# Operands of the experts' second product exchanged: activations stationary, 512 columns of the expert matrix moving, results added straight into the residual

## The reference

```python
def peer_ffn(x, wq, subkeys, u, v):
    ...
    def expert_block(args):
        xs, es, gs = args
        h = jax.nn.gelu(jnp.einsum('td,thkd->thk', xs, u[es], preferred_element_type=jnp.float32), approximate=False)
        return jnp.einsum('thk,thkd->td', gs * h, v[es].astype(jnp.float32)).astype(x.dtype)
    ...

def trunk_layer(...):
    ...
    h = h + mixed @ lp['w_out']
    h = h + peer_ffn(rms_norm(h, lp['norm2_g']), lp['peer_wq'], lp['peer_subkeys'], lp['peer_u'], lp['peer_v'])
```

## Time and profile before

| | |
|---|---|
| median of 3 runs | 5353.5 us (5353.49 to 5354.45) |
| the profiled execution: its own time, and its span | 5357.1 us, 5355.3 us |
| TensorE matmul (PE), weight loads (PEld) | 89%, 86% of the span |
| VectorE (DVE), ScalarE (ACT), GpSimd (POOL) | 59%, 31%, 7% |
| mean granted clock of TensorE, share of full speed | 0.942 |
| second product's matmuls: each of the three passes | 3584 into `ex_op` and 512 into `ex_hp` |
| adds of its outputs on VectorE (L2301) | 896 and 128, 754 ns each |

### The profile page before, as it was taken

One profiled execution on the slowest core, in us unless ns is written; L12 is line 12 of the kernel. 1 busy time (PEld: TensorE's weight loads), 2 busy tenths in 40 slices (PEclk: granted clock), 3 DMA queues, 4 the chain that ended last, 5 costly groups with the idle time before them and its releaser, 6 DMA issues. The chain is left out here.

```text
span 5355.3 us, 99808 instructions
## 1 busy us (share of the span) xinstructions
PE 4784.8 (89%) x39364; PEld 4585.4 (86%) x39364; DVE 3141.2 (59%) x6341; ACT 1671.9 (31%) x2570; POOL 363.5 (7%) x194
## 2 busy tenths in 40 slices
PE   7767697899999999999887676969999999999998
PEld 7647496899999999999885464969899999999998
DVE  3554578884555555557735644788755555555576
ACT  2322232882222222222222222228722222222222
POOL 0200054000000000000002000540000000000000
PEclk9878798999999999999988787989999999999999
DMA  3330121565333333335323301216743322333253
GB/s 96 111 140 1 54 90 53 174 198 191 115 115 127 126 115 115 129 113 177 125 78 126 117 0 71 90 44 179 214 162 125 128 115 115 128 125 115 104 196 120
DMA packets 390832, 631.24 MB, mean 118 GB/s; under 512 B 29184, under 2 KB 327680, under 8 KB 348800
## 3 DMA queue, kind: packets, MB, share of 16 engines
q1 hardware_dynamic: 388640, 620.74, 33.0%
q10 hardware_dynamic: 2016, 8.26, 0.4%
HBM read 526.52 MB, written 152.36 MB: 127 GB/s over the span
## 5 line engine op out<-in xcount | busy, mean ns | idle before, releaser
L228 PE MATMUL ex_op<-ex_ah,ex_vl 128*128 128x288 f32 x3584 | 1062.9, 297 | 7.4 <-DVE ex_acc L2301 6.4
L230 PE MATMUL ex_op<-ex_ah,ex_vh 128*128 128x288 f32 x3584 | 1058.7, 295 | 0.0
L229 PE MATMUL ex_op<-ex_al,ex_vh 128*128 128x288 f32 x3584 | 1057.8, 295 | 0.0
L2301 DVE TENSOR_TENSOR ex_acc<-ex_acc,ex_op 128x576 f32<-128x576 f32 x896 | 672.7, 754 | 549.2 <-PE ex_op L230 549.2
L228 PE MATMUL ex_hp<-x_hi,ex_ul 128*128 128x288 f32 x3072 | 906.9, 295 | 19.1 <-PEq L122 15.8
L230 PE MATMUL ex_hp<-x_hi,ex_uh 128*128 128x288 f32 x3072 | 907.3, 295 | 0.0
L229 PE MATMUL ex_hp<-x_lo,ex_uh 128*128 128x288 f32 x3072 | 906.6, 295 | 0.0
L228 PEld LDWEIGHTS ex_op<-ex_ah,ex_vl 128*128 128x128 f32 x3584 | 673.9, 188 | 14.9 <-DVE ex_acc L2301 14.9
L230 PEld LDWEIGHTS ex_op<-ex_ah,ex_vh 128*128 128x128 f32 x3584 | 674.1, 188 | 0.0
L229 PEld LDWEIGHTS ex_op<-ex_al,ex_vh 128*128 128x128 f32 x3584 | 673.9, 188 | 0.0
L2250 ACT ACTIVATE ex_vh<-ex_v 128x2048 fp32r<-128x2048 f32 x128 | 245.5, 1918 | 1139.6 <-PE ex_op L230 860.1
(11 more groups left out here) (414 smaller groups left out, 8842.7 us busy)
## 6 DMA issues: line engine op xcount, KB each, us to landing
ex_u<-in_peer_uT SPq DMA_DIRECT2D x128, 1024.0 KB, 7.7
ex_v<-in_peer_v SPq DMA_DIRECT2D x128, 1024.0 KB, 6.8
gate_matrix<-g_stage SPq DMA_DIRECT2D x18, 4096.0 KB, 15.9
ex_g<-gate_matrix SPq DMA_DIRECT2D x128, 576.0 KB, 5.0
dec_k<-in_cache_kT SPq DMA_DIRECT2D x16, 1536.0 KB, 9.7
dec_v<-in_cache_v SPq DMA_DIRECT2D x16, 1536.0 KB, 6.8
out_s_k<-in_cache_k_kept SPq DMA_DIRECT2D x128, 190.5 KB, 6.2
out_s_v<-in_cache_v_kept SPq DMA_DIRECT2D x128, 190.5 KB, 6.2
```

The source lines that it names most:

```text
L228: nc.tensor.matmul(out, w_lo, x_hi, start=first, stop=False)
L229: nc.tensor.matmul(out, w_hi, x_lo, start=False, stop=False)
L230: return nc.tensor.matmul(out, w_hi, x_hi, start=False, stop=last)
L2301: nc.vector.tensor_tensor(a, a, o[:, :, 0:HALF], ALU.add).then_inc(s.added, 1)
```

## The change

The activations become the stationary operand and V moves, 512 columns at a time. An output is now one tile of 128 tokens by 512 features: 2 expert blocks x 3 passes, 6 matmuls into one bank. There are 10 outputs per group (`OUTS`): 5 token tiles x 2 halves of the features. The last tile has 64 tokens only. For it, the low and the high part stand side by side as 128 stationary columns (`a_lo_hi`), so one matmul forms low x high in rows 0 to 63 and high x high in rows 64 to 127 of the bank, and a second, with 64 stationary columns, adds high x low to rows 0 to 63: 4 matmuls per output instead of 6. ScalarE copies the 64 columns of the high part once more for this (one more instruction per block).

VectorE adds each output, 128 x 512, directly into `h`; rows 64 to 127 of the last tile of `h` serve as the second accumulator and are set to zero at the start, in place of `acc`. At the end SyncE moves those rows to a scratch tile `lower`, and VectorE adds it to rows 0 to 63. The closing stage with its transposes is gone. The outputs go round through the four banks of `op` in both halves; `late_product` is gone, and `hp` is no longer used for outputs.

```diff
--- before.py
+++ after.py
@@ -2110,23 +2110,30 @@
 
 
     NR = NG - EARLY
+    BANKS = 4
+    OUTS = 2 * NT
     with ExitStack() as ctx:
         def sb(name, shape, dt=F32):
             return ctx.enter_context(sbuf(nc, name, shape, dt))
 
-        acc = sb("ex_acc", [P, KD, T])
+        lower = sb("ex_lower", [TS_, D])
         u_raw = [m.u_raw0, sb("ex_u", [P, KD, EG * P])]
         u_hi, u_lo = m.u_hi, m.u_lo
         early = [u[:].rearrange("p k c -> p (k c)")[:, 0:EG * T].rearrange("p (e t) -> p e t", e=EG) for u in u_raw]
         v_raw, v_hi, v_lo = (sb("ex_v" + n, [P, 2, EG, D], dt) for n, dt in (("", F32), ("h", F32R), ("l", F32R)))
         gb = sb("ex_g", [P, 2, NU, EG, UNIT])
         a_raw = sb("ex_a", [P, EG, T])
-        a_hi, a_lo = (sb("ex_a" + n, [P, 2, EG, T], F32R) for n in "hl")
+        a_hi, a_lo_hi = sb("ex_ah", [P, 2, EG, T], F32R), sb("ex_al", [P, 2, EG, T + TS_], F32R)
+        a_lo = a_lo_hi[:, :, :, 0:T]
         hp = ctx.enter_context(psum(nc, "ex_hp", [P, EG, 2, 512], F32))
-        op = ctx.enter_context(psum(nc, "ex_op", [P, 2, 2, 512], F32))
-        banks = (op[:, 0], op[:, 1], hp[:, 0], hp[:, 1])
+        op = ctx.enter_context(psum(nc, "ex_op", [P, BANKS, 512], F32))
+
+        def bank(j, n):
+
+            return (j * OUTS + n) % BANKS
+
         names = ["u_in0", "u_in1", "v_in0", "v_in1", "g_in0", "g_in1", "kept", "uh", "ul", "vh", "vl", "h_made",
-                 "gelud", "gated", "ah", "al", "out_made", "added", "zeroed", "early_in0", "early_in1"]
+                 "gelud", "gated", "ah", "al", "out_made", "added", "early_in0", "early_in1", "folded"]
         with stage(nc, *names) as (block, s):
             u_in, v_in, g_in = (s.u_in0, s.u_in1), (s.v_in0, s.v_in1), (s.g_in0, s.g_in1)
             early_in = (s.early_in0, s.early_in1)
@@ -2172,6 +2179,8 @@
                         load(i * 2 + j, j)
                 for f in range(EARLY):
                     load_early(f, f % 2)
+                sp.wait_ge(s.added, NG * OUTS)
+                sp.dma_start(lower[:], m.h[TS_:P, NT - 1, :]).then_inc(s.folded, 16)
                 sp.wait_ge(s.kept, 32 * NG)
 
             @block.tensor
@@ -2193,15 +2202,22 @@
                 def second_product(g, j, first=False):
                     pe.wait_ge(s.al, g * EG + EG)
                     pe.wait_ge(s.vl, g + 1)
-                    for n in range(KD):
-                        if not (first and n < 2):
-                            pe.wait_ge(s.added, g * KD + (n - 1))
-                        for half in range(2):
-                            t = slice(half * HALF, (half + 1) * HALF)
-                            c = slice(n * P, (n + 1) * P)
+                    for n in range(OUTS):
+                        i, c, q = n // 2, slice(n % 2 * 512, (n % 2 + 1) * 512), bank(j, n)
+                        t = slice(i * P, i * P + ROWS[i])
+                        if not (first and n < BANKS):
+                            pe.wait_ge(s.added, g * OUTS + (n - BANKS + 1))
+                        if i < NT - 1:
                             for e in range(EG):
-                                ins = three_passes(nc, op[:, n % 2, half, 0:HALF], v_hi[:, j, e, c], v_lo[:, j, e, c],
-                                                   a_hi[:, j, e, t], a_lo[:, j, e, t], e == 0, e == EG - 1)
+                                ins = three_passes(nc, op[:, q, :], a_hi[:, j, e, t], a_lo[:, j, e, t],
+                                                   v_hi[:, j, e, c], v_lo[:, j, e, c], e == 0, e == EG - 1)
+                        else:
+                            for e in range(EG):
+                                both = (op[:, q, :], a_lo_hi[:, j, e, TP_:T + TS_], v_hi[:, j, e, c])
+                                low = (op[0:TS_, q, :], a_hi[:, j, e, t], v_lo[:, j, e, c])
+                                first_e, last_e = (both, low) if e == 0 else (low, both)
+                                nc.tensor.matmul(*first_e, start=e == 0, stop=False)
+                                ins = nc.tensor.matmul(*last_e, start=False, stop=e == EG - 1)
                         ins.then_inc(s.out_made, 1)
 
                 first_product(0, 0, True)
@@ -2214,26 +2230,9 @@
                     second_product(i * 2, 0)
                 second_product(NR - 1, 1)
 
-                def late_product(g, j, first=False):
-
-                    pe.wait_ge(s.al, g * EG + EG)
-                    pe.wait_ge(s.vl, g + 1)
-                    for n in range(KD):
-                        if not (first and n in (2, 3)):
-                            pe.wait_ge(s.added, g * KD + (n - (1 if first and n < 2 else 3)))
-                        for half in range(2):
-                            t = slice(half * HALF, (half + 1) * HALF)
-                            c = slice(n * P, (n + 1) * P)
-                            for e in range(EG):
-                                ins = three_passes(nc, banks[n % 4][:, half, 0:HALF], v_hi[:, j, e, c], v_lo[:, j, e, c],
-                                                   a_hi[:, j, e, t], a_lo[:, j, e, t], e == 0, e == EG - 1)
-                        ins.then_inc(s.out_made, 1)
-
-                late_product(NR, 0, True)
-                late_product(NR + 1, 1)
-                with pe.Fori(NR // 2 + 1, NG // 2) as i:
+                with pe.Fori(NR // 2, NG // 2) as i:
                     for j in range(2):
-                        late_product(i * 2 + j, j)
+                        second_product(i * 2 + j, j)
 
             @block.scalar
             def _(act):
@@ -2246,11 +2245,12 @@
                 def split_v(g, j, turn, first=False):
                     act.wait_ge(v_in[j], turn * 16 + 16)
                     if not first:
-                        act.wait_ge(s.out_made, g * KD - KD)
+                        act.wait_ge(s.out_made, g * OUTS - OUTS)
                     nc.scalar.activation(v_hi[:, j], v_raw[:, j], ACT.Copy).then_inc(s.vh, 1)
 
                 def high(g, j, e):
                     act.wait_ge(s.gated, g * EG + (e + 1))
+                    nc.scalar.activation(a_lo_hi[:, j, e, T:T + TS_], a_raw[:, e, TP_:T], ACT.Copy)
                     nc.scalar.activation(a_hi[:, j, e, :], a_raw[:, e, :], ACT.Copy).then_inc(s.ah, 1)
 
                 def step(g, j, turn, first=False, last=False):
@@ -2293,12 +2293,11 @@
                     nc.vector.tensor_tensor(v_lo[:, j], v_raw[:, j], v_hi[:, j].bitcast(F32),
                                             ALU.subtract).then_inc(s.vl, 1)
 
-                def add(g, ns, late=False):
+                def add(g, j, ns):
                     for n in ns:
-                        dve.wait_ge(s.out_made, g * KD + (n + 1))
-                        a = acc[:, n, :].rearrange("p (a t) -> p a t", a=2)
-                        o = banks[n % 4] if late else banks[n % 2]
-                        nc.vector.tensor_tensor(a, a, o[:, :, 0:HALF], ALU.add).then_inc(s.added, 1)
+                        dve.wait_ge(s.out_made, g * OUTS + (n + 1))
+                        hh = m.h[:, n // 2, n % 2 * 512:(n % 2 + 1) * 512]
+                        nc.vector.tensor_tensor(hh, hh, op[:, bank(j, n), :], ALU.add).then_inc(s.added, 1)
 
                 def gate(j, e, h):
                     nc.vector.tensor_tensor(a_raw[:, e, :].rearrange("p (u t) -> p u t", u=NU),
@@ -2320,12 +2319,12 @@
                         if e == 0:
                             split_v(g, j)
                         elif not first:
-                            add(g - 1, (0,))
+                            add(g - 1, 1 - j, (0,))
                         low(g, j, e)
                     if not first:
-                        add(g - 1, range(1, KD))
-
-                def early_step(g, j, turn, f_turn, first=False):
+                        add(g - 1, 1 - j, range(1, OUTS))
+
+                def early_step(g, j, turn, f_turn):
                     dve.wait_ge(g_in[j], turn * 16 + 16)
                     dve.wait_ge(early_in[j], f_turn * 16 + 16)
                     dve.wait_ge(s.al, g * EG)
@@ -2334,10 +2333,9 @@
                     split_v(g, j)
                     for e in range(EG):
                         low(g, j, e)
-                    add(g - 1, range(KD), not first)
-
-                nc.vector.memset(acc[:], 0.0).then_inc(s.zeroed, 1)
-                dve.wait_ge(s.zeroed, 1)
+                    add(g - 1, 1 - j, range(OUTS))
+
+                nc.vector.memset(m.h[TS_:P, NT - 1, :], 0.0)
                 dve.sem_inc(s.ul, 1)
                 step(0, 0, 0, first=True)
                 step(1, 1, 0)
@@ -2346,32 +2344,14 @@
                     step(i * 2 + 1, 1, i)
                 step(NR - 2, 0, NR // 2 - 1)
                 step(NR - 1, 1, NR // 2 - 1, last=True)
-                early_step(NR, 0, NR // 2, 0, True)
+                early_step(NR, 0, NR // 2, 0)
                 early_step(NR + 1, 1, NR // 2, 0)
                 with dve.Fori(NR // 2 + 1, NG // 2) as i:
```

(24 more changed lines are left out.)

## The result

| | before | after |
|---|---|---|
| median of 17 runs each | 5353.4 us (5349.2 to 5359.6) | 5363.5 us (5354.7 to 5369.9) |
| the profiled execution, and its span | 5357.1, 5355.3 | 5364.1, 5362.3 |

The ratio is 1.0018 with a 95% interval of 1.001 to 1.0025: a little slower, 10.1 us, at the upper edge of what the prediction counted as no change (10.7). It lies in the predicted range, and 6.8 us above the predicted 5356.7. The two profiled executions differ by 7.0.

What follows compares the result with a forecast made beforehand. TensorE's matmul pace was taken to bound the first half, with VectorE's order of work also mattering in the late half. Terms −5 + 24 − 7 − 9 = +3 us on the 5353.5 median gave 5356.7 us; range 5346 to 5380.

Steps and rivals of the forecast that it cites:

- Late half: Late groups: four banks hold 5.44 us of work, so TensorE waits for VectorE, 1.12 us per group instead of 0.31; +24 us.
- First boundary: First late boundary of each layer: costs 1.12 us like the others instead of 4.76; −7 us over both layers.
- Close: End of each layer's expert stage: a fold of 6.3 us replaces closes of 9.7 and 11.7; −9 us.
- The row of 2.9 us for another transfer: Close: moving 256 KB to the scratch tile taken as 2.9 us from the nearest row, bounds 2 to 6 us.
- Streaming: Second products in all groups: 12.71 us each with the swapped operands against 12.75; −5 us in all.
- 128 × (−0.04): The multiplication for second products: 0.04 us saved in each group, over 64 groups and 2 layers; −5 us.
- A change of width: Rival: two switches per group from 64 to 128 stationary columns each stall 0.13 us; +33 us, 5390; chance 0.08.
- Columns do not count alone: Denies the rival that second products' time scales with columns only, 13.22 us each; +60 us, 5417; chance 0.03.
- 40 loads fewer are worth little: Second products: fewer weight loads gain little where a load is hidden behind the matmul before it; no separate size.
- The clock rival: Rival: late-half waits let TensorE drop to 1.2 GHz; 46 us, 5403, or 5380 if every second falls; chance 0.09.
- the late wait would not grow: Rival: VectorE reaches the late adds 0.8 us sooner or TensorE needs the bank later; 24 us vanish, 5332; chance 0.06.

Runs made afterwards that it cites:

- experiment 1: The changed kernel with five PSUM banks instead of four for late-half outputs, the fifth from `hp`: 5326.4 us, ratio 0.995 to the kernel before.
- experiment 2: Late-half adds of outputs 0, 1 and 2 moved ahead of the low parts: in the changed kernel 5327.4 us, in the kernel before 5337.3 us.
- experiment 4: The changed kernel with full tiles' outputs made in two pieces of 256 moving columns, 96 matmuls for 48: 5428.6 us, ratio 1.0138.
- experiment 6: The changed kernel of experiment 2, with the 64-token tile first in each group and the fold's transfer started earlier: 5315.9 us, ratio 0.993.

## Why the prediction was right, and where it was off

- **Late half: right.** The wait, its place, its releaser and its moment came out as worked out: t = 5.49 and 6.23 at ten of the sixteen boundaries of each layer, and 0.1 later at the other six. Experiments 1 and 2 remove the wait from either side, by room and by order, and the time falls by 37 and 36 us; by the periods (13.89 and 12.71) it should be 30 × 1.18 = 35 in the first, which keeps its two first boundaries, and 32 × 1.18 = 38 in the second. The term was a little small: 25.3 with its streaming, for 22.8. About 1.1 of that is the 0.1 us by which the gates start later at those six (12 × 0.09 in both layers); the prediction carried one price for all.
- **First boundary: right**, −7.5 for −7. In experiment 1 it still shows the cost of a four-bank boundary, 13.84.
- **Close: right**, −8.4 for −9. The row of 2.9 us for another transfer served: the fold's add was released 2.90 after the last add.
- **Streaming: mis-sized.** The step "128 × (−0.04)" holds only where second products follow one another: with the waits gone, their periods are 12.75 and 12.71 (experiment 2). It fails in the first half, 96 of the 128 groups, where they alternate with first products. TensorE's timeline, the first matmul of a second product and of the first product behind it, in the kernel before (two lines) and after:

```profile
1503.36 0.29 PE L228 MATMUL ex_op<-ex_ah,ex_vl 128*128 128x288 f32 x1
1516.10 0.29 PE L228 MATMUL ex_hp<-x_hi,ex_ul 128*128 128x288 f32 x1
1503.50 0.39 PE L228 MATMUL ex_op<-ex_vh,ex_al 128*128 128x512 f32 x1
1516.24 0.29 PE L228 MATMUL ex_hp<-x_hi,ex_ul 128*128 128x288 f32 x1
```

Both take 12.74. A pair of products takes 25.453 us after the change (fifteen from the split of V at 1516.44 to that at 1898.24) against 25.467 before (1516.30 to 1898.30): 0.014 gained, not 0.04. Over 96 groups that is −1.3. The two layers show −0.6 and −2.2. The 1.5 that layer 1 has more is not streaming: in the profiled execution of the kernel before, an idle of 1.89 us at the start of that stage was followed by a clock of 0.50 (TensorE's timeline and a stretch), and from the second split of V to the third it took 20.59 us, for 19.05 in layer 0:

```profile
3899.52 0.37 PE L228 MATMUL ex_hp<-x_hi,ex_ul 128*128 128x288 f32 x1 [1.89 <-ACT ex_a L2264]
3900.00:3903.00 3.00, 3.00 (x15) 3.00 (x14) 3.00 (x3) 1.23 (x2) 0.00 (x0) 0.50 0.38 158
```

- **The rest of the 10.1.** The rows explain 6.6 of the profiled pair's 7.0. The other 3 us between the medians lie in the choice of the pair: the profiled execution of the kernel before is 3.7 us above its median, that of the change 0.6. Of this, 1.5 is the slow start just shown; I can't assign the rest. Stages that the change doesn't touch scatter by as much: in the profiled executions of these nine kernels, the first split of V in layer 0 starts anywhere from 1230.3 to 1236.9.
- **The rivals.** A change of width costs nothing (0.230 per step, above). Columns do not count alone: experiment 4 finds 13 ns per matmul beside them. For the same reason the prediction's remark that 40 loads fewer are worth little does not hold: the 40 matmuls with their loads are worth 0.53 us per group, and the added columns take most of it back. The clock rival needs a longer wait than this change makes; its condition was put as "nearer 1.6 than 1", and the waits were 0.83 to 0.93. Its price was put at 1.4 us a boundary and is about 1.6. That the late wait would not grow was wrong; it becomes true only with experiment 1 or 2.

## What to carry to other kernels

When outputs get smaller, count what the free PSUM banks hold in microseconds of TensorE's work and set it against the longest stretch in which the evicting engine does something else; here 5.44 us stood against a little over 6. If it doesn't fit, evictions can be moved forward into the long block: three of them moved were worth as much here as another bank (36 and 37 us). In this case the cost of the operand exchange was then a short sum: columns times their pace, plus a fixed part per matmul, plus what the new layout does at the end.

## What was not expected of the hardware

- The same idle mechanism at two lengths has very different prices: at 0.83 us it costs itself and 0.16 of restart (the period of 13.86 from 5199.00 to 5212.86, less 12.71 and the 0.99 by which the fifth output came late), at 2.36 us it costs itself and, in 31 cases of 32, about 1.6 more, because the granted clock then stands at 0.50 for some 3 us. No run was made for the lengths between. Single idles at the start of the expert stages lie there: 1.67 us in experiment 6 (layer 1) left the clock at 1.00, 1.89 us in the kernel before (layer 1) and 2.31 us in experiment 2 (the change, layer 0) were followed by 0.50.
- The branch at the end of VectorE's loop seems to show at the boundary: 0.70 instead of 0.60 between two instructions in every second group. The delay first shows at the fifth boundary of each layer, the first one behind a turn of that loop. That it is the branch was not tried.
